# Projecting and normalising token slabs inside the attention loop of a two-layer mixer block

## Chip, cores and metric

One Trainium2 chip, all 8 cores. Each core computes one batch element with the same program; there is no traffic between cores. The metric is the device time of the slowest core in microseconds.

## What is computed

Two layers over x of 2048 tokens by 1024 features per batch element. Only the end of the first half of a layer matters here:

```python
for i in range(DEPTH):
    h = rms_norm(x, norm1_w[i])
    proj = h @ w_in[i]
    ...
    yd = diff_attn_mixer(pd, ...)        # causal, 4 heads, two score maps per head
    mix = jnp.concatenate([ya, yb, yc, yd], axis=-1)
    x = x + mix @ w_out[i]
    h = rms_norm(x, norm2_w[i])
    x = x + (silu(h @ ffn_w_gate[i]) * (h @ ffn_w_up[i])) @ ffn_w_down[i]
```

The differential attention takes, per head, two softmax maps p0 and p1 (32 features each for q and k), forms p0 - lam * p1, applies it to v (64 features), and normalises the result over each head's 64 features. Its 256 output features are the last quarter of `mix`.

## The kernel before

Everything is held transposed, features on partitions: xT (8 chunks of 128 features by 2048 tokens, fp32), hT (the normalised input, bf16) and mixT (bf16). Tokens are worked in four slabs of 512 (`NS = 4`). A layer goes through five mixer stages, then the projection by w_out with the second norm, then the FFN. Each engine runs its instructions in the order in which the program emits them; `Prog.op` works out the semaphore waits from the tiles read and written. For PSUM it takes whole 2 KB banks, whoever writes or reads them (`ap_region`).

PSUM has eight banks: psA has six, pst two. In the attention stage the scores rotate over `Sbanks` (L857: psA 0, psA 1, and half of pst), the accumulator of a head is psA 2 or 3 in turn (L887), psA 4 and 5 take the transposed outputs, and pst holds the sums and the transposes of the epilogue.

The attention stage is a list of units (L858 on): eight query blocks of 256 tokens (`qs`), in each four heads, in each the key blocks of 128 that the causal mask and the bias leave over. `emit_S` (L870) puts a unit's scores on TensorE: one matmul of 512 columns (two maps by 256 queries), and one more that adds the mask on the diagonal. `emit_exp_pv` (L883) has ScalarE take the exponential into SBUF, and TensorE multiply it with v into the head's bank; behind a head's last unit the bank is copied out, by ScalarE for even heads and VectorE for odd ones. The loop keeps two units ahead: unit u+2 has its scores emitted before unit u is retired (`retire`, L940). Later work of a head is put off by a count of retired units: three after its last unit its output is transposed (`emit_oT_transposes`, L893, 16 small transposes), and behind the fourth head's come `epilogue_a` (L901, a chain over VectorE and GpSimd) for the two 128-query blocks and, six units later, `epilogue_b` (L916: two transposes and a ScalarE copy into mixT).

The projection follows (L965 on): for each slab and each of 8 output chunks, 8 matmuls of 512 columns into one of six rotating banks (`psbank`, L419), and a VectorE add into xT. One slab behind it goes `norm_slab` (L452): 8 squares on ScalarE through two buffers, 8 matmuls with a matrix of ones, a logarithm, an exponential, and 8 VectorE multiplies into hT. The norm of the last slab is emitted behind that of the slab before it.

The FFN's weights come by GpSimd's queue in pieces (`load_group`, L988; slots of `load_piece`). The projection's two weight halves `pO` lie in slots 0 and 1, so the first gate piece (slot 0) waits for the last matmul on the first half, and the first up piece (slot 1) for the projection's last matmul. `ffn_gu` computes 8 gate matmuls and then 8 up matmuls per block of 128.

Of the kernel before, what the change touches and what calls it, by code (L numbers as in the profile page):

```python
# [11 lines left out]
AF = mybir.ActivationFunctionType  # L12
ALU = mybir.AluOpType
# [229 lines left out]
D = 1024  # L243
L = 2048
NT = 16
NS = 4
# [3 lines left out]
EPS = 1e-6  # L250
# [5 lines left out]
CP_N1W, CP_N2W, CP_CONVW, CP_CONVB, CP_DCOL, CP_SSMNW, CP_PSCALE, CP_QNW, CP_KNW, CP_BS = 0, 8, 16, 40, 46, 48, 50, 52, 53, 54  # L256
# [60 lines left out]
def build(nlayers=2, dbg=(), stop=None):  # L317
# [23 lines left out]
    def sb(name, shape, dt):  # L341
        return es.enter_context(nc.sbuf_tensor("s_" + name, list(shape), dt))
# [4 lines left out]
    P = Prog(nc, sem)  # L347

    xT = sb("xT", [128, 8, L], F32)
    hT = sb("hT", [128, 8, L], BF16)  # L350
    mixT = sb("mixT", [128, 8, L], BF16)
    arena = sb("arena", [128, ARENA], U8)
    cF = sb("cF", [128, NCF], F32)
    colp = sb("colp", [128, NCOLP], F32)
# [5 lines left out]
    onesb = sb("onesb", [128, 128], BF16)  # L360
    neghalf = sb("neghalf", [128, 1], F32)
    small = sb("small", [128, 64], F32)
    psA = es.enter_context(nc.psum_tensor("psA", [128, 6, 512], F32))
# [26 lines left out]
    def load_piece(slot, src, ncols, kind="in"):  # L390
        dst = ring_slot(slot, kind)
        if kind == "in":
            dst = dst[:, :, 0:ncols]
        else:
            dst = dst[:, 0:ncols, :]
        P.dma('pool', dst, src, 'ring%d' % slot, writes_sb=[dst])
        return dst
# [21 lines left out]
    def psbank(lo=0, hi=6):  # L419
        k = (lo, hi)  # L420
        v = psrot.get(k, 0)
        psrot[k] = v + 1
        return lo + v % (hi - lo)

    def load_x(fuse_norm):
        bm = Bump(arena, 16384, ARENA)
        stage = [bm.alloc([128, D], F32) for _ in range(4)]
        nbx = norm_bufs() if fuse_norm else None
        for t in range(NT):
            st = stage[t % 4]  # L430
            P.dma('sp', st, x_d[t * 128:(t + 1) * 128, :], 'xin%d' % (t % 4), writes_sb=[st])
            for half in range(2):
                b = psbank()
                for c4 in range(4):
                    c = half * 4 + c4
                    P.transpose(psA[:, b, c4 * 128:(c4 + 1) * 128], st[:, c * 128:(c + 1) * 128], identf)
                src = psA[:, b, :].rearrange("p (c t) -> p c t", c=4)
                dst = xT[:, half * 4:half * 4 + 4, t * 128:(t + 1) * 128]
                P.copy('act' if (t + half) % 2 == 0 else 'dve', dst, src)
            if fuse_norm and t % 4 == 3 and t >= 7:  # L440
                norm_slab(t // 4 - 1, CP_N1W, nbx)
        if fuse_norm:
            norm_slab(NS - 1, CP_N1W, nbx)

    def norm_bufs():
        bm = Bump(arena, 50 * 1024, ARENA)
        sq = [bm.alloc([128, 512], BF16) for _ in range(2)]
        ms = bm.alloc([128, 512], F32)
        rs = bm.alloc([128, 512], F32)
        return sq, ms, rs  # L450

    def norm_slab(s, nw_off, bufs):  # L452
        sq, ms, rs = bufs
        sl = slice(s * 512, (s + 1) * 512)
        b = psbank()
        for c in range(8):
            P.act(sq[c % 2], xT[:, c, sl], AF.Square)
            P.mm(psA[:, b, :], onesb[:], sq[c % 2], start=(c == 0), stop=(c == 7))
        P.act(ms, psA[:, b, :], AF.Ln, scale=1.0 / D, bias=EPS)
        P.act(rs, ms, AF.Exp, scale=-0.5)  # L460
        for c in range(8):
            P.stt(hT[:, c, sl], xT[:, c, sl], colp[:, nw_off + c:nw_off + c + 1], rs, ALU.mult, ALU.mult)

    def norm_full(nw_off):
        bufs = norm_bufs()
        for s in range(NS):
            norm_slab(s, nw_off, bufs)
# [23 lines left out]
    def layer(li, pre_normed=False):  # L491
# [95 lines left out]
        for cc in range(2):  # L587
            for s in range(NS):
                b = psbank()
                proj_fm(pC, cc * 128, s, b)  # L590
                P.copy('act', pcxs[cc][:, 16 + s * 512:16 + (s + 1) * 512], psA[:, b, :])
        for cc in range(2):
# [19 lines left out]
            for s in range(NS):  # L612
                sl = slice(s * 512, (s + 1) * 512)
                b = psbank()
# [46 lines left out]
        for zc in range(2):  # L661
            for s in range(NS):
                b = psbank()
# [166 lines left out]
        for blk in range(4):  # L830
            for s in range(NS):
                sl = slice(s * 512, (s + 1) * 512)
                b = psbank(0, 3)
# [12 lines left out]
        for t in range(NT):  # L846
            b = psbank()
            for dc in range(8):
# [3 lines left out]
        pO = [load_piece(0, w_out_d[li][:, 0:512].rearrange("(c p) n -> p c n", p=128), 512),  # L852
              load_piece(1, w_out_d[li][:, 512:1024].rearrange("(c p) n -> p c n", p=128), 512)]
# [29 lines left out]
        def emit_exp_pv(u, b):  # L883
            qs, h, kb, first, last = u
            e = 2 * qs - kb + 1
            P.act(PT[b], Sbanks[b], AF.Exp, bias=cF[:, CF_ALIBI + h * 17 + e:CF_ALIBI + h * 17 + e + 1])
            ob = 2 + (qs * 4 + h) % 2  # L887
            P.mm(psA[:, ob, :], vflat[:, kb, h * 65:h * 65 + 128], PT[b], start=first, stop=last)
            if last:
                ot = oTs[(qs * 4 + h) % 2]  # L890
                P.copy('dve' if h % 2 else 'act', ot[0:65, :], psA[0:65, ob, :])

        def emit_oT_transposes(qs, h):  # L893
            ot = oTs[(qs * 4 + h) % 2]
            for c in range(2):
                for j in range(2):
                    cols = slice(c * 256 + j * 128, c * 256 + (j + 1) * 128)
                    P.transpose(psA[:, 4 + j, (c * 4 + h) * 64:(c * 4 + h + 1) * 64], ot[0:64, cols], identf[0:64, 0:64])
                    P.transpose(psSum[:, j * 8 + c * 4 + h:j * 8 + c * 4 + h + 1], ot[64:65, cols], identf[64:65, 64:65])

        def epilogue_a(qb):  # L901
            j = qb % 2
            onb = onbs[j]
            P.recip(rc, psSum[:, j * 8:(j + 1) * 8])
            P.ts('dve', nr1, rc[:, 4:8], neglam, None, op0=ALU.mult)
            P.tt('dve', h4(o0), h4(psA[:, 4 + j, 0:256]), rc[:, 0:4].unsqueeze(2).to_broadcast([128, 4, 64]), ALU.mult)
            P.tt('dve', h4(o1), h4(psA[:, 4 + j, 256:512]), nr1.unsqueeze(2).to_broadcast([128, 4, 64]), ALU.mult)
            P.tt('pool', o0, o0, o1, ALU.add)
            P.tt('dve', o1, o0, o0, ALU.mult)
            P.rsum(ss4, h4(o1))  # L910
            P.ts('dve', ss4, ss4, 1.0 / 64, EPS, op0=ALU.mult, op1=ALU.add)
            P.tt('pool', rs4, ss4, neghalf[:, 0:1].to_broadcast([128, 4]), ALU.pow)
            P.tt('dve', h4(o1), h4(o0), rs4.unsqueeze(2).to_broadcast([128, 4, 64]), ALU.mult)
            P.stt(onb, o1, 1.0 - lam_init, rowp[:, RP_SUBLN:RP_SUBLN + 256], ALU.mult, ALU.mult)

        def epilogue_b(qb):  # L916
            ql = slice(qb * 128, (qb + 1) * 128)
            j = qb % 2
            ts0 = j * 2
            for jj in range(2):  # L920
                P.transpose(pst[:, ts0 + jj, :], onbs[j][:, jj * 128:(jj + 1) * 128], identb[:])
            P.copy('act', mixT[:, 6:8, ql], pst[:, ts0:ts0 + 2, :])

        pend = []
        deferred = []

        def fire(item):
            _, kind, args = item
            if kind == 'T':
                qs_, h_ = args  # L930
                emit_oT_transposes(qs_, h_)
                if h_ == 3:
                    epilogue_a(2 * qs_)
                    epilogue_a(2 * qs_ + 1)
                    deferred.append([6, 'E', 2 * qs_])
                    deferred.append([6, 'E', 2 * qs_ + 1])
            else:
                epilogue_b(args)

        def retire():  # L940
            pu, pb = pend.pop(0)
            emit_exp_pv(pu, pb)
            for d in deferred:
                d[0] -= 1
            ready = [d for d in deferred if d[0] <= 0]
            for d in ready:
                deferred.remove(d)
                fire(d)
            if pu[4]:
                deferred.append([3, 'T', (pu[0], pu[1])])  # L950

        for u in units:
            pend.append((u, emit_S(u)))
# [3 lines left out]
            retire()  # L957
        while deferred:
            fire(deferred.pop(0))

        if stop != 'D':
            dump('mix%d' % li, mixT)
# [1 line left out]

        nb = norm_bufs()  # L965
        for s in range(NS):
            sl = slice(s * 512, (s + 1) * 512)
            for c in range(8):
                half, cj = c // 4, c % 4
                b = psbank()  # L970
                for mc in range(8):
                    P.mm(psA[:, b, :], pO[half][:, mc, cj * 128:(cj + 1) * 128], mixT[:, mc, sl], start=(mc == 0), stop=(mc == 7))
                P.tt('dve', xT[:, c, sl], xT[:, c, sl], psA[:, b, :], ALU.add)
            if s >= 1:
                norm_slab(s - 1, CP_N2W, nb)
        norm_slab(NS - 1, CP_N2W, nb)

        dump('x1_%d' % li, xT)
        chk('wout')
# [174 lines left out]
```

How the kernel before makes its waits and increments, by code:

```python
        def run(engname, e):  # L157
            for waits, thunk, tok in plan[engname]:
                if thunk is None:
                    for s, v in waits:
                        e.wait_ge(semh[s], v)
                    continue
                for s, v in waits[:-1]:
                    e.wait_ge(semh[s], v)
                ins = thunk(e)
                if waits:
                    s, v = waits[-1]
                    ins._wait_ge(semh[s], v)
                if tok is None:
                    pass
                elif tok[0].startswith('d_'):
                    ins.then_inc(semh[tok[0]], 16)
                else:
                    ins.then_inc(semh[tok[0]], 1)
```

## Time and profile before

| | |
|---|---|
| time of three runs, median (lowest to highest) | 2531.61 us (2528.35 to 2532.37) |
| the profiled execution, time | 2531.23 us |
| its span on the slowest core | 2529.5 us |
| spans of the eight cores | 2520.7 to 2529.5 us |
| busy: TensorE / VectorE / ScalarE / GpSimd | 83% / 39% / 34% / 11% |
| mean granted clock of TensorE, slowest core | 0.893 |
| attention loop of the first layer | from about 427 to 719 us |
| projection and second norm of the first layer | from 724.4 to 800.7 us |

The slowest core's profile is read. Times in it count from the span's start. A clock of 1.00 is 2.4 GHz and 0.50 is 1.2 GHz. Durations come from the profiled execution. In the chain of waits a row is a start, a length and what the chain was in; a PE row's count is of matmuls in a row. "L197" is the helper through which all matmuls go, L212 that of ScalarE's activations, L215 and L225 those of VectorE and GpSimd element-wise operations, L201 that of transposes.

### The profile page before, as it was taken

The numbers are of one execution on the slowest core, as the hardware profiler recorded it, in microseconds if no ns is written. First come the engines' busy times: TensorE is split into PE (matmuls) and PEld (weight loads), VectorE is DVE, ScalarE is ACT, GpSimd is POOL, SyncE is SP. The second block draws the span as 40 slices with busy tenths as digits, with TensorE's granted clock in tenths as the row PEclk, the third lists the DMA queues.
The fourth block names the chain that finished last, engine by engine and source line by source line (L and its number), as shares of the span: only waits on it lengthen the run. The fifth ranks groups of instructions, "written<-read, shape, count | busy, mean of one in ns | idle before, by whom it ended". The sixth has DMA issues, their size and how long they took to land.

```text
span 2529.5 us, 26176 instructions; the slowest of 8 cores (2520.7 to 2529.5 us)
## 1 busy us (share of the span) xinstructions
PE 2091.8 (83%) x9828; PEld 926.2 (37%) x9828; DVE 986.1 (39%) x1912; ACT 870.4 (34%) x1512; POOL 281.2 (11%) x430
## 2 busy tenths in 40 slices
PE   5659558877879999999965875687787999999997
PEld 3224334322333444444322344243222344444443
DVE  3740563212125333333467136422111443333344
ACT  3524445456733111111143343545674211111111
POOL 0620320101000000000016023010000000000000
PEclk7869769788889999999988886878898999999999
DMA  6020102000006213210102010010000243221103
GB/s 172 1 35 1 26 1 34 0 1 1 0 1 92 46 19 50 46 22 9 28 1 34 1 26 1 10 24 1 0 1 0 29 71 51 36 43 23 26 1 133
DMA packets 56655, 69.19 MB, mean 27 GB/s; under 512 B 5456, under 2 KB 46416, under 8 KB 56528
## 3 DMA queue, kind: packets, MB, share of 16 engines
q0 software_dynamic: 51200, 49.63, 13.4%
q1 hardware_dynamic: 5328, 17.88, 2.0%
q8 instruction: 77, 1.26, 0.2%
q14 instruction: 50, 0.41, 0.1%
HBM read 108.75 MB, written 8.39 MB: 46 GB/s over the span
## 4 chain that ended last, share of the span: by engine, by line
PE 71%; DVE 13%; ACT 6%; POOL 5%; issue 3%; DMA 1%; SPq 0%; DVEq 0%; ACTq 0%; POOLq 0%
PE psA L197 65%; ACT s_arena L212 6%; DVE s_arena L215 5%; POOL s_arena L215 3%; DVE s_arena L225 3%; PE psA L201 3%; PE pst L201 2%; PE pst L197 2%; POOL s_small L215 1%; DVE s_hT L225 1%; DVE s_xT L215 1%; DMA s_arena<-x 1%; DVE s_small L237 1%; DVE s_small L221 1%; DMA out<-s_arena 0%
## 5 line engine op out<-in xcount | busy, mean ns | idle before, releaser
L197 PE MATMUL psA<-s_hT,s_arena 128*128 128x512 bf16 x3712 | 840.0, 385 | 2.3 <-ACT s_arena L212 2.3
L197 PE MATMUL psA<-s_arena 128*128 128x512 bf16 (+3 forms) x1662 | 401.9, 358 | 168.5 <-POOL s_arena L215 85.6
L197 PEld LDWEIGHTS psA<-s_hT,s_arena 128*128 128x128 bf16 x3712 | 367.8, 99 | 448.9 <-issue 23.4
L212 ACT ACTIVATE s_arena<-psA 128x512 bf16<-128x512 f32 (+1 forms) x354 | 210.0, 593 | 904.8 <-PE psA L197 904.7
L197 PE MATMUL psA<-s_mixT,s_arena 128*128 128x512 bf16 x1920 | 451.5, 386 | 13.4 <-DVE s_xT L215 12.8
L215 DVE TENSOR_TENSOR s_xT<-s_xT,psA 128x512 f32<-128x512 f32 x448 | 304.2, 687 | 120.6 <-PE psA L197 114.5
L215 DVE TENSOR_TENSOR s_mixT<-s_arena,psA 128x512 bf16<-128x512 bf16 x176 | 121.0, 688 | 479.4 <-PE psA L197 476.5
L197 PEld LDWEIGHTS psA<-s_arena 128*128 128x128 bf16 (+1 forms) x1662 | 128.1, 109 | 416.3 <-ACT s_arena L212 191.1
L197 PEld LDWEIGHTS psA<-s_mixT,s_arena 128*128 128x128 bf16 x1920 | 166.1, 99 | 288.6 <-DVE s_xT L215 125.2
L212 ACT ACTIVATE s_arena<-psA,s_cF 128x512 bf16<-128x512 f32 x352 | 228.8, 693 | 51.6 <-PE psA L197 51.2
L215 POOL TENSOR_TENSOR s_arena<-s_arena 128x256 f32<-128x256 f32 (+2 forms) x160 | 118.6, 742 | 733.1 <-DVE s_arena L215 666.8
L231 DVE COPY s_arena<-psA 65x512 f32<-65x512 f32 (+2 forms) x50 | 33.5, 670 | 376.3 <-PE psA L197 359.8
L197 PE MATMUL psA<-s_arena,s_onesb 128*128 128x512 bf16 x144 | 67.6, 492 | 84.5 <-ACT s_arena L212 79.9
L212 ACT ACTIVATE s_arena<-pst,s_cF 128x512 bf16<-128x512 f32 x174 | 120.5, 693 | 44.8 <-PE pst L197 44.6
L201 PE MATMUL psA<-s_cF,s_arena 64*128 64x64 f32 (+1 forms) x384 | 102.2, 323 | 27.5 <-DMA s_arena<-x 18.4
L212 ACT ACTIVATE s_arena<-s_arena 128x512 f32<-128x512 f32 (+2 forms) x150 | 92.0, 614 | 76.2 <-DVE s_arena L215 71.2
L212 ACT ACTIVATE s_arena<-s_xT 128x512 bf16<-128x512 f32 x128 | 73.3, 621 | 130.2 <-PE psA L197 119.3
L225 DVE SCALAR_TENSOR_TENSOR s_hT<-s_xT,s_colp,s_arena 128x512 bf16<-128x512 f32 x128 | 86.2, 747 | 72.6 <-ACT s_arena L212 72.6
L201 PE MATMUL pst<-s_identb,s_arena 128*128 128x128 bf16 x256 | 37.4, 259 | 90.0 <-DVE s_arena L225 69.2
L197 PE MATMUL psA<-s_arena,s_hT 128*128 128x512 bf16 (+2 forms) x768 | 97.5, 276 | 7.0 <-DVE s_arena L215 5.0
L201 PEld LDWEIGHTS psA<-s_cF,s_arena 64*128 64x128 f32 (+1 forms) x384 | 59.2, 163 | 56.9 <-issue 39.6
L142 POOL DMA_DIRECT2D s_arena<-ffn_w_gate x12 | 10.8, 898 | 595.7 <-PE psA L197 595.7
(82 smaller groups left out, 1310.0 us busy)
## 6 DMA issues: line engine op xcount, KB each, us to landing
s_arena<-ffn_w_gate POOLq DMA_DIRECT2D x10, 1024.0 KB, 10.3
s_arena<-ffn_w_up POOLq DMA_DIRECT2D x10, 1024.0 KB, 13.6
s_arena<-ffn_w_down POOLq DMA_DIRECT2D x10, 1024.0 KB, 8.3
s_arena<-x SPq DMA_DIRECT2D x16, 512.0 KB, 8.0
s_arena<-w_in POOLq DMA_DIRECT2D x8, 1024.0 KB, 9.9
out<-s_arena SPq DMA_DIRECT2D x16, 512.0 KB, 2.7
s_arena<-w_out POOLq DMA_DIRECT2D x4, 1024.0 KB, 8.6
s_arena<-w_in POOLq DMA_DIRECT2D x4, 512.0 KB, 11.9
```

The lines of the kernel that those rows point to most:

```text
L142: self.plan[queue].append((waits, (lambda e, o=out, i=in_, k=kw: e.dma_start(out=o, in_=i, **k)), tok))
L197: return self.op('pe', lambda e: e.matmul(out, lhsT, rhs, start=start, stop=stop, **kw), reads=[lhsT, rhs], writes=[out])
L201: return self.op('pe', lambda e: e.transpose(out, in_, ident), reads=[in_, ident], writes=[out])
L212: return self.op('act', lambda e: e.activation(out, in_, func, **kw), reads=rd, writes=[out])
L215: return self.op(eng, lambda e: e.tensor_tensor(out, in0, in1, op), reads=[in0, in1], writes=[out])
L221: return self.op(eng, lambda e: e.tensor_scalar(out, in0, s1, s2, op0, **kw), reads=[in0, s1, s2], writes=[out])
L225: return self.op('dve', lambda e: e.scalar_tensor_tensor(out, in0, scalar, in1, op0, op1), reads=[in0, scalar, in1], writes=[out])
L231: return self.op(eng, lambda e: e.tensor_copy(out, in_), reads=[in_], writes=[out])
L237: return self.op('dve', lambda e: e.reduce_sum(out, in_, AX.X), reads=[in_], writes=[out])
```

## The change

With `interleave` on (it is, in the full program), the projection of slabs 0 to 2 and their second norm are emitted inside the attention loop. Once `epilogue_b` has written the last block of a slab, nine items are queued: eight `wout_unit` (8 matmuls, one VectorE add) and one `norm_slab_inplace`. At each retired unit that isn't the last of its head, one item is taken and emitted behind the unit's value matmul. Its bank is the accumulator bank that the current head doesn't use. The norm takes its two square buffers from hT's last slab and writes logarithm and exponential in place in the PSUM bank, since the arena's norm buffers lie under the attention's tiles. Slab 3 is projected and normalised behind the loop as before.

```diff
-    def norm_slab(s, nw_off, bufs):
+    def norm_slab(s, nw_off, bufs, bank=None):
         sq, ms, rs = bufs
         sl = slice(s * 512, (s + 1) * 512)
-        b = psbank()
+        if bank is None:
+            bank = psA[:, psbank(), :]
...
+        interleave = stop is None
+        fill = []
+        wout_done = set()
+        fill_bank = [None]
+
+        def wout_unit(s_, c, bank=None):
+            sl = slice(s_ * 512, (s_ + 1) * 512)
+            half, cj = c // 4, c % 4
+            if bank is None:
+                bank = fill_bank[0]
+            for mc in range(8):
+                P.mm(bank, pO[half][:, mc, cj * 128:(cj + 1) * 128], mixT[:, mc, sl], start=(mc == 0), stop=(mc == 7))
+            P.tt('dve', xT[:, c, sl], xT[:, c, sl], bank, ALU.add)
+
+        def norm_slab_inplace(s_, nw_off, bank):
+            assert s_ < NS - 1
+            sl = slice(s_ * 512, (s_ + 1) * 512)
+            sq = [hT[:, 0, (NS - 1) * 512:NS * 512], hT[:, 1, (NS - 1) * 512:NS * 512]]
+            for c in range(8):
+                P.act(sq[c % 2], xT[:, c, sl], AF.Square)
+                P.mm(bank, onesb[:], sq[c % 2], start=(c == 0), stop=(c == 7))
+            P.act(bank, bank, AF.Ln, scale=1.0 / D, bias=EPS)
+            P.act(bank, bank, AF.Exp, scale=-0.5)
+            for c in range(8):
+                P.stt(hT[:, c, sl], xT[:, c, sl], colp[:, nw_off + c:nw_off + c + 1], bank, ALU.mult, ALU.mult)
+
+        def enqueue_slab(s_):
+            for c in range(8):
+                fill.append(lambda s_=s_, c=c: wout_unit(s_, c))
+            fill.append(lambda s_=s_: norm_slab_inplace(s_, CP_N2W, fill_bank[0]))
+            wout_done.add(s_)
...
                 epilogue_b(args)
+                if interleave and args % 4 == 3 and args // 4 < NS - 1:
+                    enqueue_slab(args // 4)
...
             if pu[4]:
                 deferred.append([3, 'T', (pu[0], pu[1])])
+            elif fill:
+                fill_bank[0] = psA[:, 2 + (pu[0] * 4 + pu[1] + 1) % 2, :]
+                fill.pop(0)()
...
+        while fill:
+            fill_bank[0] = psA[:, psbank(0, 4), :]
+            fill.pop(0)()
...
         for s in range(NS):
-            sl = slice(s * 512, (s + 1) * 512)
+            if s in wout_done:
+                continue
             for c in range(8):
-                half, cj = c // 4, c % 4
-                b = psbank()
-                for mc in range(8):
-                    P.mm(psA[:, b, :], pO[half][:, mc, cj * 128:(cj + 1) * 128], mixT[:, mc, sl], start=(mc == 0), stop=(mc == 7))
-                P.tt('dve', xT[:, c, sl], xT[:, c, sl], psA[:, b, :], ALU.add)
-            if s >= 1:
-                norm_slab(s - 1, CP_N2W, nb)
-        norm_slab(NS - 1, CP_N2W, nb)
+                wout_unit(s, c, bank=psA[:, psbank(), :])
+            norm_slab(s, CP_N2W, nb)
```

## Rows read from the trace of the kernel before

**Rows 1.** The page: busy time by engine, and the chain's shares.
```profile
PE 2091.8 (83%) x9828; PEld 926.2 (37%) x9828; DVE 986.1 (39%) x1912; ACT 870.4 (34%) x1512; POOL 281.2 (11%) x430
...
PE 71%; DVE 13%; ACT 6%; POOL 5%; issue 3%; DMA 1%; SPq 0%; DVEq 0%; ACTq 0%; POOLq 0%
```
**Rows 2.** Windows, first layer: busy time by engine, clock, DMA share, GB/s.
```profile
427.00:719.00 292.00, 230.28 (x872) 91.06 (x871) 54.88 (x153) 174.28 (x293) 26.59 (x31) 0.82 0.03 4
724.00:730.00 6.00, 5.96 (x17) 2.27 (x18) 0.69 (x1) 1.00 (x2) 0.00 (x0) 0.53 0.00 0
730.00:755.00 25.00, 25.00 (x117) 11.17 (x115) 9.88 (x15) 0.67 (x2) 0.00 (x0) 1.00 0.00 1
755.00:760.00 5.00, 3.70 (x14) 1.27 (x14) 0.43 (x1) 4.49 (x9) 0.00 (x0) 1.00 0.01 2
...
798.00:805.00 7.00, 6.70 (x15) 2.06 (x16) 5.62 (x10) 5.18 (x8) 0.00 (x0) 0.52 1.09 157
805.00:815.00 10.00, 10.00 (x48) 4.51 (x46) 5.07 (x8) 1.55 (x3) 0.00 (x0) 1.00 1.14 165
```
**Rows 3.** The chain of waits in a steady part of the loop.
```profile
646.13 0.22 PE pst L197
646.35 1.52 PE psA L197 x5
```
**Rows 4.** The chain of waits around an epilogue, at the end of query block 1.
```profile
482.36 0.44 DVE s_arena L225
...
482.94 0.39 PE pst L201 x2
...
486.52 2.13 PE psA L197 x5
```
**Rows 5.** Windows around the same epilogue, columns as in rows 2.
```profile
478.00:484.00 6.00, 0.98 (x6) 0.49 (x4) 2.59 (x8) 0.97 (x3) 1.74 (x2) 0.71 0.00 0
484.00:491.00 7.00, 7.00 (x21) 3.01 (x21) 0.69 (x1) 4.38 (x7) 0.00 (x0) 0.52 0.00 0
```
**Rows 6.** The chain of waits in the projection stage of the first layer.
```profile
724.41 30.31 PE psA L197 x128
...
754.74 0.70 DVE s_xT L215
755.44 0.05 issue
...
758.38 14.22 PE psA L197 x65
...
790.48 0.03 issue
...
800.69 14.47 PE psA L197 x57
```
**Rows 7.** Timeline of GpSimd: the issue of the first up piece.
```profile
790.77 0.87 POOL L142 DMA_DIRECT2D s_arena<-ffn_w_up  x1 [5.97 <-PE psA L197]
```
**Rows 8.** Landing of that piece, alone, and in the second layer (shortest of two).
```profile
DMA to landing us min/median/max: 12.0/12.0/12.0
...
DMA to landing us min/median/max: 12.2/15.0/17.8
```
**Rows 9.** The chain of waits in the projection stage of the second layer.
```profile
1948.46 29.28 PE psA L197 x128
...
2015.19 0.02 issue
...
2025.10 15.00 PE psA L197 x57
```
**Rows 10.** Timeline: one matmul of the loop, and the end of a norm.
```profile
645.97 0.38 PE L197 MATMUL pst<-s_arena 128*128 128x512 bf16 x1
...
758.81 0.60 ACT L212 ACTIVATE s_arena<-psA 128x512 f32<-128x512 f32 x1 [0.48 <-PE psA L197]
759.44 0.63 ACT L212 ACTIVATE s_arena<-s_arena 128x512 f32<-128x512 f32 x1
...
760.18 5.39 DVE L225 SCALAR_TENSOR_TENSOR s_hT<-s_xT,s_colp,s_arena 128x512 bf16<-128x512 f32 x8 [4.75 <-ACT s_arena L212]
```

More of the change, by code:

```diff
@@ L450, in norm_bufs @@
         return sq, ms, rs
-    def norm_slab(s, nw_off, bufs):
+    def norm_slab(s, nw_off, bufs, bank=None):
         sq, ms, rs = bufs
         sl = slice(s * 512, (s + 1) * 512)
-        b = psbank()
+        if bank is None:
+            bank = psA[:, psbank(), :]
         for c in range(8):
             P.act(sq[c % 2], xT[:, c, sl], AF.Square)
-            P.mm(psA[:, b, :], onesb[:], sq[c % 2], start=(c == 0), stop=(c == 7))
-        P.act(ms, psA[:, b, :], AF.Ln, scale=1.0 / D, bias=EPS)
+            P.mm(bank, onesb[:], sq[c % 2], start=(c == 0), stop=(c == 7))
+        P.act(ms, bank, AF.Ln, scale=1.0 / D, bias=EPS)
         P.act(rs, ms, AF.Exp, scale=-0.5)
@@ L925, in layer @@
         deferred = []
+        interleave = stop is None
[16 more added lines that the diff above has]
+                P.act(sq[c % 2], xT[:, c, sl], AF.Square)
+                P.mm(bank, onesb[:], sq[c % 2], start=(c == 0), stop=(c == 7))
+            P.act(bank, bank, AF.Ln, scale=1.0 / D, bias=EPS)
[7 more added lines that the diff above has]
+            wout_done.add(s_)
         def fire(item):
```

## The prediction

> **What bounds the kernel now.** I first read the page's totals and its chain of waits: TensorE (PE) is busy 83% of the span and carries 71% of the chain, so PE time, or time in which PE is made to wait, is what the end depends on [rows 1]. The windows then split the part of a layer that the change touches. The first layer's attention loop is 292 us long; in it PE is busy 230.3 us, ScalarE (ACT) 174.3 us, and the granted clock averages 0.82. The output projection after it runs at 117 matmuls in 25 us, 0.2137 us each, at the full 2.4 GHz [rows 2]. So the loop has 61.7 us without PE work, and the question is where they lie.
>
> The chain of waits and the timeline show two kinds of gap. In the steady loop the chain carries a score and a value matmul for each unit (one head, one block of 128 keys), six in 1.74 us, 0.58 us a unit, where two matmuls at 0.2137 take 0.43 [rows 3]. The rest, 0.15 us a unit, is PE waiting for the exponential. The long gaps are elsewhere: at the end of each pair of 128-query blocks, PE stands for about 5 us (0.98 us busy of 6) until VectorE (DVE) and GpSimd (POOL) have finished the second block's epilogue and its transposes start at 482.94 us [rows 4, 5]. After it the clock is at 1.2 GHz, and the chain has five matmuls in 2.13 us, 0.427 each [rows 4, 5].
>
> **What the change takes out.** Slabs 0 to 2 (512 tokens each) leave the stage behind attention. Before, the 128 matmuls of two slabs take 30.31 us from 724.41, and the projection's last matmul ends at 790.48; the norms of slabs 0 and 1 lie between [rows 6]. The last two norms then hold PE until 800.69, where the FFN starts, still at 1.2 GHz (0.52 in that window) [rows 2, 6]. Eight gate matmuls at 0.427 bring its first up matmul to about 804.1.
>
> After, slab 3 alone is left: 64 matmuls, the first 5.3 us of them at 1.2 GHz as in rows 2 (0.53 over 6 us), so about 16.3 us, ending at 724.4 + 16.3 = 740.7. One norm follows, about 4 us. But the FFN's second weight piece goes to the slot that the projection's last matmul reads. POOL issues it at 790.77, 0.29 us behind that matmul, and it lands 12.0 us later [rows 7, 8]. The first up matmul can start at 740.7 + 12.3 = 753.0 at the earliest, with PE idle from about 746.5. So **removing the norm of slab 2 from the end frees little: the transfer was hidden by two norms and now is not.** I add 2.1 us for a low clock after this idle time (before, the next window after 804 is at full speed). Saved: 804.1 − 753.0 − 2.1 = 49.0 us. In the second layer, by the same steps, the projection starts at 1948.46, ends at 2015.19, the piece lands 12.2 us after its issue, and the FFN starts at 2025.10 [rows 8, 9]; the low clock at the projection's start is shorter (29.28 us for its 128 matmuls), which makes about 50.5 us. **Together 99.5 us off.** SP's queue is not touched; POOL's epilogue work keeps its place, and its loads only move forward with the projection.
>
> **What it puts in.** The units retire in order, and every one that isn't the last of its head takes one fill. Counting them by the code (8, 16, 24, 31, 37, 43, 49 and 55 units for the eight query blocks of 256, numbered from 0): slab 0 is queued at unit 32, slab 1 at unit 87, slab 2 at unit 167, each right *behind* the long gap of its epilogue. Nine fills follow at once; none meets one of the 5 us gaps. So the matmuls fill only the 0.15 us a unit.
>
> (a) Eight groups of 8 matmuls per slab: 64 × 0.2137 = 13.7 us. All fills of a head use one bank, the other accumulator's. So the next group waits until DVE has added the last one: a matmul takes 0.38 us to its end, then 0.02, 0.70 for the add, 0.05 [rows 6, 10]. From one group's first matmul to the next: 7 × 0.2137 + 0.38 + 0.77 = 2.65 us; the ten matmuls of a fill and a unit are 2.14, which leaves 0.51; I take 0.56, as a weight load can stand in front. Six of the eight fills per slab wait so (one has the eight transpose pairs of the previous head before it, one is the first): 3.4 us. In slab 0 two of these waits are for the output copy of the head before, of the same size. Against it: eight bubbles of 0.15 filled, 1.2 us, and about 0.5 us once because ACT still has two scores ahead. Sum 13.7 + 3.4 − 1.7 = 15.4 us a slab, **46 us a layer**. Bounds: no waits at all, 36; waits and no bubbles, 52.
>
> Rows 2 show this stage with six rotating banks at 0.2137 us a matmul, no wait between groups. The Trainium skill (Perfetto Trace Analysis, Matmuls) says that independent groups should rotate through banks so that the evacuation overlaps the next group's matmuls. The change gives that up; were it kept, the sum would be 3 × 3.4 × 2 = 20 us lower, 2557. The bound "no waits at all" already covers this from the rows.
>
> (b) A norm in the loop. In the projection stage the ACT squares lie beside its matmuls except for about 4 us: from 754.74 to 758.38, where the ones-matmuls and the squares go to and fro over two buffers. The two activations after it (0.60, 0.63) and DVE's eight multiplies (5.39) lie beside the next slab's matmuls [rows 6, 10]. In the loop ACT runs in order: the next unit's exponential is queued behind all of it, PE's value matmul waits for that exponential, and the later scores wait behind it on PE. From the last fill: 1.2 to 1.9 us until the bank is free, 4.0, the last matmul's end 0.4, 1.3 for logarithm and exponential, 0.6 for the unit's own; about 8.1, of which three units (1.7 us) were there before: 6.4, and 5.8 where the bank is free sooner: **18.6 us a layer**. Bounds 15 and 20. No table is loaded: logarithm and exponential follow the squares and each other within 0.5 us, with no load between [rows 10]. Writing both back into PSUM in place is in no row; 0.60 us from PSUM to SBUF and 0.63 within SBUF are nearest, so I take them.
>
> (c) The bank stays held until DVE's eight multiplies end, 5.4 us. In slabs 0 and 2 the next head needs that bank after 6 and 5 units, 3.5 and 2.9 us: 2.0 + 2.6 = 4.6 us. In slab 1 it is ten units away: nothing. The head's DVE copy queues behind the multiplies, which lies in the same wait.
>
> (d) The clock. After ACT has held PE for 6 us with eight matmuls in them, it may fall, as it does after two norms (0.52 from 798 to 805) though not after one (1.00 from 755 to 760) [rows 2]. After an epilogue some 10 us go at 1.2 GHz (0.71 over 6 us, 0.52 over the next 7) [rows 5]; they hold 11.7 units of 0.854 us, which take 6.8 at full speed: 3.2 us. For (c) and (d) together between 3 and 14; I take **8 us a layer**, the drop in about half of the cases with the wait of (c) shorter then. That the fills begin at a low clock costs about 2 us a slab, and about as much returns, since dense matmuls end that stretch sooner: nothing, bounds −2 and +3 a slab.
>
> **Sum:** 2 × (46 + 18.6 + 8) = 145.2 in, 99.5 out, +46 us. The profiled execution took 2531.2 us (span 2529.5), 0.4 below the median of the three runs, 2531.6; so 2577.5.
>
> **Rivals.** *The gaps swallow the matmuls (faster).* If (a) cost nothing, because PE's 61.7 idle us a layer take up the 46, only (b), (c) and (d) remain: 2 × 26.6 − 99.5 = −46, 2485. The point from which it decides: the loop grows by less than 49.8 us a layer. For it: the idle time is large enough [rows 2]; against it: most of it lies at the epilogues, where no fill is taken. The Trainium skill (Perfetto Trace Analysis, Optimization Strategy) says that interleaving regimes whose busiest engine differs may improve performance; that rule would have this rival right. Chance 0.10.
> *The clock stays low around the fills.* Each norm fill drops it, and the groups after the epilogue run long at 1.2 GHz: 14 for (c) and (d), 3 × 3 more for the starts, 2 × (46 + 18.6 + 23) − 99.5 = +76, 2607. For it: every epilogue gap in the loop is followed by such a stretch. Chance 0.15.
> *The costs only just cancel:* 48 to 52 us more in each loop, by a shorter wait in (a) and no drop in (d). 2531, chance 0.04.
> *The norm at the end hides the transfer after all:* if the piece landed as late as before or earlier counted from the projection's end, my 49 would move by 5 us a layer at most; it is inside the range and gets no chance of its own.
> My forecast has 0.71.
>
> **Numbers.** Low end: (a) 43, (b) 15, (c, d) 3, twice, less 101, gives +21, 2552. High end: the clock rival, 2607. Faster by over 0.2% (5 us, about what a measurement tells from no change) has the first rival's 0.10; slower has the forecast and the clock rival, 0.86.
>
> **What would show it.** Right: attention stages of about 365 us instead of 292; PE waiting for DVE's adds into xT some 0.5 us about six times a slab; three gaps of PE of 4 to 6 us a layer behind squares; the FFN's first up matmul 12.3 us behind the projection's last one, with PE idle before it; the 5 us epilogue gaps as they were. Wrong: loops under 340 us, or fills that fall into epilogue gaps, or no wait for the second FFN piece.

## The result, and the profile after

The changed kernel takes **2584.68 us** (median of 9 runs) against 2532.55 us before (10 runs): a ratio of 1.022, interval 1.0195 to 1.0245. It is slower, by 52 us, where 46 were forecast. Some runs of most kernels, in which the granted clock of a die is lower, are longer by some per cent; they are in the medians, but not in the ratios, here and below. The profiled execution took 2586.25 us with a span of 2584.7 us.

The page of the changed kernel: span, busy time by engine, the chain by engine, then three groups of the costliest (busy time and mean ns, and behind the last bar the idle time before them).

```profile
span 2584.7 us, 26167 instructions; the slowest of 8 cores (2572.4 to 2584.7 us)
PE 2116.5 (82%) x9828; PEld 930.7 (36%) x9828; DVE 987.9 (38%) x1912; ACT 875.1 (34%) x1512; POOL 281.7 (11%) x430
PE 69%; DVE 14%; ACT 6%; POOL 5%; issue 3%; DMA 2%; SPq 0%; DVEq 0%; ACTq 0%; POOLq 0%
...
L197 PE MATMUL psA<-s_hT,s_arena 128*128 128x512 bf16 x3712 | 838.2, 384 | 14.1 <-DMA s_arena<-ffn_w_up 13.0
...
L197 PE MATMUL psA<-s_mixT,s_arena 128*128 128x512 bf16 x1920 | 468.9, 392 | 24.7 <-DVE s_xT L215 21.5
...
L212 ACT ACTIVATE s_arena<-psA,s_cF 128x512 bf16<-128x512 f32 x352 | 230.7, 692 | 108.4 <-PE psA L197 107.8
```

Against [rows 1], PE's count of instructions is the same and its share no higher. New are 13.0 us in which the FFN's matmuls wait for the up pieces. The wait of the projection's matmuls for VectorE's adds into xT is now 21.5 us; it was 12.8 before. ScalarE now waits 108 us for scores, 52 before.

**Where the time went.** The ScalarE copies that end each epilogue are marks that both traces have. Three of them are these, of the changed kernel (start, length, what, idle before it), with PE's transposes that the first waits for:

```profile
540.19 0.37 PE L201 MATMUL pst<-s_identb,s_arena 128*128 128x128 bf16 x2 [4.97 <-DVE s_arena L225]
...
540.66 0.37 ACT L230 COPY s_mixT<-pst 128x256 bf16<-128x256 bf16 x1 [5.03 <-PE pst L201]
...
750.99 0.37 ACT L230 COPY s_mixT<-pst 128x256 bf16<-128x256 bf16 x1 [4.85 <-PE pst L201]
...
799.26 0.37 ACT L230 COPY s_mixT<-pst 128x256 bf16<-128x256 bf16 x1 [4.74 <-PE pst L201]
```

The brackets show the 5 us gap of the epilogue, on PE 4.97 us, as long as ever: no fill fell into it. The times between the second copy of one query block of 256 and the next, in the first layer, for the kernels that follow as well (slab 0 is taken in the first stretch, slab 1 in the third, slab 2 in the fifth):

| from epilogue | before | changed | no_add | spaced | norm_out | gap_plain |
|---|---|---|---|---|---|---|
| 1 to 2 | 31.5 | 57.7 | 54.1 | 52.6 | 47.7 | 31.2 |
| 2 to 3 | 35.0 | 36.9 | 36.9 | 35.9 | 36.8 | 35.6 |
| 3 to 4 | 39.1 | 62.5 | 59.5 | 60.7 | 53.3 | 38.5 |
| 4 to 5 | 41.6 | 41.5 | 41.3 | 42.0 | 40.9 | 39.2 |
| 5 to 6 | 46.1 | 69.5 | 69.0 | 66.2 | 59.4 | 45.1 |
| 6 to 7 | 47.8 | 48.3 | 48.3 | 48.2 | 47.8 | 47.8 |
| sum over before | | +75.2 | +68.0 | +64.5 | +44.8 | −3.7 |
| the same, second layer | | +77.5 | +70.5 | +67.6 | +48.6 | −3.0 |

The first layer's loop grows by 75.2 us (77.5 in the second), 26.3, 23.4 and 23.4 us of it in the three stretches that take a slab, and the rest behind the first.

**Inside a stretch.** The chain of waits of the changed kernel, second slab: group, add, group.

```profile
585.20 0.70 DVE s_xT L215
585.90 0.05 issue
585.94 1.91 PE psA L197 x8
587.86 0.02 issue
587.88 0.70 DVE s_xT L215
588.58 0.05 issue
588.63 1.91 PE psA L197 x8
```

A period is 588.63 − 585.94 = 2.69 us. VectorE's add is on the chain in each, since the next group goes to the same bank. PE's visible idle time for it is 0.35 us a time, 16 times in the first layer's loop. In the projection stage before, with six banks, it was beside PE's work [rows 6].

The norm in the loop, third slab: the end of its chain, with ScalarE, then VectorE's eight multiplies, then PE.

```profile
708.69 0.62 ACT s_hT L212
709.31 0.04 issue
709.36 0.40 PE psA L197
709.76 0.02 issue
709.78 0.59 ACT psA L212
710.37 0.02 issue
710.40 0.59 ACT psA L212
...
711.09 5.37 DVE s_hT L225 x8
716.46 0.14 issue
716.59 1.24 PE psA L197 x5
```

The two activations in place in PSUM take 0.59 us each. The next head's first value matmul waits until the multiplies are through with its bank; PE is idle for 2.62 us there. Behind the squares PE has no single long gap: it stands for 0.44 us before the first ones-matmul, 0.51 and twice 0.20 us between them, and 1.45 us before its next value matmul.

**The end.** The chain from the projection of slab 3 to the FFN, first layer:

```profile
799.17 16.65 PE psA L197 x65
815.81 0.07 issue
815.89 12.41 DMA s_arena<-ffn_w_up
...
828.44 3.66 PE psA L197 x9
```

Before, the FFN's first matmuls, in the first and in the second layer, are these:

```profile
801.09 5.22 PE L197 MATMUL psA<-s_hT,s_arena 128*128 128x512 bf16 x15
...
2026.03 4.37 PE L197 MATMUL psA<-s_hT,s_arena 128*128 128x512 bf16 x10
```

Eight of them at 0.427 us are gate matmuls, so the first up matmul starts at 804.5 and 2029.4. From the projection's start to it is 29.3 us now, 80.1 before; in the second layer 2080.41 − 2051.66 = 28.8, before 81.0. That is 103.0 us saved in both. In: 75.2 + 77.5 = 152.7. The difference, about 50, is most of the 55 us between the two profiled executions. Of the rest, 2.5 us are the last transfer of the output, 5.19 us long instead of 2.70, and the low clock behind the two waits for the up pieces costs 3 to 4 us, an estimate from the clock over four microseconds behind each (0.67 from 829, 0.50 from 2080). Windows in the first layer:

```profile
817.00:829.00 12.00, 4.24 (x15) 1.52 (x16) 5.39 (x8) 5.32 (x8) 3.03 (x4) 0.82 0.97 131
829.00:833.00 4.00, 4.00 (x14) 1.49 (x12) 0.69 (x1) 0.00 (x0) 0.00 (x0) 0.67 1.06 168
```

(Changed kernel, columns as in rows 2: PE has 4.24 us of work in 12, and the granted clock is 0.67 in the four behind.)

### The profile page after: what moved, and what is told of

Same layout as the page of the kernel before. It is cut to its first block, busy times and chain, and to the rows that moved or that the text cites. A ratio compares the mean times of both kernels' runs of the same rounds, so it can differ in the third digit from the quotient of the medians.

```text
span 2584.7 us, 26167 instructions; the slowest of 8 cores (2572.4 to 2584.7 us)
## 1 busy us (share of the span) xinstructions
PE 2116.5 (82%) x9828; PEld 930.7 (36%) x9828; DVE 987.9 (38%) x1912; ACT 875.1 (34%) x1512; POOL 281.7 (11%) x430
## 4 chain that ended last, share of the span: by engine, by line
PE 69%; DVE 14%; ACT 6%; POOL 5%; issue 3%; DMA 2%; SPq 0%; DVEq 0%; ACTq 0%; POOLq 0%
PE psA L197 63%; DVE s_arena L215 5%; ACT s_arena L212 5%; POOL s_arena L215 3%; DVE s_arena L225 3%; PE psA L201 3%; PE pst L201 2%; DVE s_xT L215 2%; PE pst L197 2%; DVE s_hT L225 1%; POOL s_small L215 1%; DMA s_arena<-ffn_w_up 1%; DMA s_arena<-x 1%; DVE s_small L237 1%; DVE s_small L221 1%
## 5 line engine op out<-in xcount | busy, mean ns | idle before, releaser
L197 PE MATMUL psA<-s_arena 128*128 128x512 bf16 (+3 forms) x1662 | 411.2, 362 | 179.9 <-POOL s_arena L215 88.4
L197 PE MATMUL psA<-s_mixT,s_arena 128*128 128x512 bf16 x1920 | 468.9, 392 | 24.7 <-DVE s_xT L215 21.5
L201 PE MATMUL psA<-s_cF,s_arena 64*128 64x64 f32 (+1 forms) x384 | 103.8, 327 | 26.3 <-DMA s_arena<-x 17.8
L201 PE MATMUL pst<-s_identb,s_arena 128*128 128x128 bf16 x256 | 37.7, 261 | 89.0 <-DVE s_arena L225 69.5
L197 PE MATMUL psA<-s_arena,s_onesb 128*128 128x512 bf16 x96 | 47.3, 520 | 75.3 <-ACT s_arena L212 72.3
L197 PE MATMUL pst<-s_arena 128*128 128x512 bf16 x174 | 76.5, 440 | 0.0
L215 DVE TENSOR_TENSOR s_arena<-s_arena 128x256 f32<-128x256 f32 (+4 forms) x72 | 54.3, 754 | 52.7 <-POOL s_arena L215 29.0
L225 DVE SCALAR_TENSOR_TENSOR s_hT<-s_xT,s_colp,s_arena 128x512 bf16<-128x512 f32 x80 | 53.9, 746 | 52.6 <-ACT s_arena L212 52.6
```

The source lines that it names most:

```text
L197: return self.op('pe', lambda e: e.matmul(out, lhsT, rhs, start=start, stop=stop, **kw), reads=[lhsT, rhs], writes=[out])
L201: return self.op('pe', lambda e: e.transpose(out, in_, ident), reads=[in_, ident], writes=[out])
L215: return self.op(eng, lambda e: e.tensor_tensor(out, in0, in1, op), reads=[in0, in1], writes=[out])
L225: return self.op('dve', lambda e: e.scalar_tensor_tensor(out, in0, scalar, in1, op0, op1), reads=[in0, scalar, in1], writes=[out])
```

## The experiments

All are measured beside the kernel before. The ratios are of the same session's runs. The kernel before took 2531.9 to 2533.0 us in each session, so times of different sessions can be set beside each other.

**no_add: the adds left out.** Slabs 0 to 2 don't get the projected mix here.

```diff
-            P.tt('dve', xT[:, c, sl], xT[:, c, sl], bank, ALU.add)
+            if s_ == NS - 1:
+                P.tt('dve', xT[:, c, sl], xT[:, c, sl], bank, ALU.add)
```

> The VectorE adds of the projection into xT are left out for slabs 0 to 2 (so these tokens miss the projected mix); everything else is as changed. If the wait of the second group of a head for the one shared bank costs what I priced (six waits of about 0.56 us a slab, three slabs, two layers), this run is 20 us faster than the changed kernel, about 2565 us. Rival, that the matmuls as such don't fit between the exponentials and the wait for the bank only stands where PE would wait for ScalarE anyway: under 5 us faster. Rival, that the clock sets the extra time: the denser matmuls should bring it up, and more than 25 us go.

Measured: 2569.31 us, ratio 1.0135 (1.0083 to 1.0187), 15.4 us less than the changed kernel. The wait is real and on the path, smaller than priced. By the table the first layer's stretches of slabs 0 and 1 get 3.6 and 3.0 us shorter, near the price (3.4), that of slab 2 only 0.5; in the second layer slabs 0 and 1 give 3.2 and 4.5 us, and slab 2 takes 2.1 us more. The clock moved at the same time. These are the 12 us behind the norm of slab 2, in no_add (first row) and in the changed kernel (second):

```profile
699.00:711.00 12.00, 10.72 (x32) 4.49 (x33) 1.74 (x3) 6.34 (x10) 0.00 (x0) 0.57 0.00 0
```
```profile
716.50:728.50 12.00, 10.86 (x41) 4.17 (x42) 0.54 (x1) 8.87 (x15) 0.00 (x0) 0.86 0.00 0
```

During the norm itself the clock is 1.00 in both. Behind it no_add runs at 0.57 and gets 32 matmuls done in 12 us where the changed kernel, at 0.86, gets 41. In the stretch of slab 0 it is the other way round: mean clock 0.82 in no_add, 0.77 in the changed kernel. Only in that of slab 1 is it nearly the same, 0.87 and 0.88, and there the waits cost 3.0 us.

**norm_out: the norms out of the loop**, those of slabs 0 and 1 ahead of the projection of slab 3.

```diff
-            fill.append(lambda s_=s_: norm_slab_inplace(s_, CP_N2W, fill_bank[0]))
...
+        norm_slab(0, CP_N2W, nb)
+        norm_slab(1, CP_N2W, nb)
+        for c in range(8):
+            wout_unit(NS - 1, c, bank=psA[:, psbank(), :])
+        norm_slab(2, CP_N2W, nb)
+        norm_slab(3, CP_N2W, nb)
```

> Only the projections stay in the loop; the norms of slabs 0 and 1 are emitted behind the loop ahead of the projection of slab 3, the norm of slab 2 behind it, ahead of that of slab 3. My theory: out of the loop go 18.6 us (ScalarE held) and about 8 us (bank held, clock) a layer; behind it come two norms of about 5 us each that nothing hides, and the third stands in time that is spent waiting for the second FFN piece. So about 16 us a layer less than the changed kernel, 2552 us. Rival, that the norms cost nothing in the loop (ScalarE had spare time there): about 20 us more than the changed kernel, 2605 us.

Measured: 2546.78 us, ratio 1.0057 (1.0029 to 1.0086), 38 us less than the changed kernel, where 32 were expected. The loop now grows by 44.8 us in the first layer and 48.6 in the second, which is the price of the projection groups alone (46 forecast); the norms are the other 30.4 and 28.9 us (26.6 forecast). Behind the loop the two norms hold PE for about 12 us that nothing hides, 769.46 to 781.47; in the chain of norm_out, ScalarE and PE take turns:

```profile
770.50 0.62 PE psA L197
771.14 0.64 ACT s_arena L212
771.78 0.05 issue
```

and the projection of slab 3 begins at 781.47. It is still better than norms in the loop, where the attention's own exponentials stand behind them.

**spaced: a fill at every second unit.**

```diff
             elif fill:
-                fill_bank[0] = psA[:, 2 + (pu[0] * 4 + pu[1] + 1) % 2, :]
-                fill.pop(0)()
+                fill_gap[0] += 1
+                if fill_gap[0] % 2:
+                    fill_bank[0] = psA[:, 2 + (pu[0] * 4 + pu[1] + 1) % 2, :]
+                    fill.pop(0)()
```

> A fill at every second unit that may take one, instead of at every one. PE's added work is the same; the adds now lie under a whole unit, and ScalarE can run ahead. My theory: a fill adds about 1.4 us instead of 2.1, so 18 waits of 0.56 us and some bubbles a layer come back: 20 to 28 us less than the changed kernel, 2557 to 2565 us. Rival, that every fill costs its 8 matmuls whatever the distance: within 5 us of the changed kernel.

Measured: 2563.24 us, ratio 1.0114 (1.0044 to 1.0184), 21 us less than the changed kernel, the forecast's near end. The loop is 10.7 and 9.9 us shorter in the two layers, more than leaving out the adds gave (7.2 and 7.0). In its chain the groups and units run on, 11 and 13 matmuls without a wait, and the add shows only where a head ends:

```profile
581.31 2.39 PE psA L197 x11
583.72 0.70 DVE s_xT L215
...
584.56 2.96 PE psA L197 x13
```

**up_first: the order of the FFN's first pieces.** The up piece is issued first and goes into the third weight slot.

```diff
+            if gi == 0:
+                wu = load_piece(2, wu_d[li][:, 0:n * 128].rearrange("(c p) n -> p c n", p=128), n * 128)
+                wg = load_piece(0, wg_d[li][:, 0:n * 128].rearrange("(c p) n -> p c n", p=128), n * 128)
+                wd = load_piece(1, wd_d[li][0:n * 128, :].rearrange("(j p) n -> p j n", p=128), n, kind="down")
+                return wg, wu, wd
```

> The first up piece of the FFN goes into the third weight slot, free since the attention ended, and is issued first; the down piece takes the slot that the projection's last matmul frees. My theory: the wait of PE for that piece (12.4 us from the projection's last matmul, about 7 us of it idle) goes, and with it the low clock after it: 7 to 9 us a layer, 2567 to 2571 us. Rival, that the gate piece, issued later in this order and sharing the DMA engines, then lands as late: under 4 us in all.

Measured: 2565.75 us, ratio 1.0125 (1.0082 to 1.0168), 18.9 us less than the changed kernel, about 1 us more than the expected range. In the first layer the gate piece is now the transfer in the chain, but PE is idle for only 0.53 us before it, where it was idle for 7.1 us before the up piece; in the second layer PE waits for neither:

```profile
809.17 11.07 DMA s_arena<-ffn_w_gate
...
820.38 3.40 PE psA L197 x15
```

**before_up: the same order in the kernel before.** Edit as above.

> The kernel before the change, with the order of the FFN's first pieces of up_first: the up piece first, into the third slot. In up_first this took 18.9 us off the changed kernel. My theory: the wait for that piece exists only since the norm of slab 2 no longer stands between the projection's end and the FFN, so here it gains nothing, 2529 to 2535 us. Rival, that the order of the pieces is worth something in any case (a calmer DMA queue at the FFN's start): 2515 to 2525 us.

Measured: 2531.85 us against 2531.9, ratio 1.000 (0.9989 to 1.001). The order of the pieces is worth nothing where two norms stand between the projection and the FFN. The 18.9 us are a wait that the change made: 13.0 us of them are the idle time that the page shows, and part of the rest is the low clock behind it.

**gap_plain: groups at the epilogues instead of at the units.** The fill at each retired unit is dropped, three groups are taken at each epilogue of query blocks 2 to 6, the nine left over follow the loop, and the tail is that of norm_out. The edit, without `take_fills`, which takes a group for each bank it is given:

```diff
             for d in ready:
                 deferred.remove(d)
+                if d[1] == 'E':
+                    if d[2] % 2 == 0:
+                        take_fills([psA[:, 2 + (pu[0] * 4 + pu[1] + 1) % 2, :]])
+                    else:
+                        take_fills([psA[:, 4, :], psA[:, 5, :]])
                 fire(d)
```

> As norm_out, but the projection groups of slabs 0 to 2 are no longer taken one per unit. Three are taken at each epilogue of the query blocks 2 to 6: one ahead of the first epilogue transposes, in the spare accumulator bank, and two ahead of the second ones, in the two banks of the transposed outputs, which the epilogue has read by then. The nine that are left follow the loop. My theory: PE stands for 1.6 and 4.8 us there whatever happens, so these 15 groups a layer cost next to nothing, and the nine behind the loop 1.7 us each with several banks: 46 us a layer become about 16, so 60 us less than norm_out, 2487 us, less a few more where the denser matmuls keep the clock up. Rival, that the adds queued on VectorE behind the epilogue, and the next head's transposes behind them, give most of it back: 2525 to 2545 us.

Measured: 2479.06 us, ratio 0.9789 (0.9769 to 0.9809): 68 us less than norm_out, 53 less than the kernel before. In the loop 15 groups a layer cost less than nothing, −3.7 us (second layer −3.0). The timeline of PE at the epilogue of query block 2 shows the three groups, and only 0.76 us of the gap are left:

```profile
505.02 1.89 PE L197 MATMUL psA<-s_mixT,s_arena 128*128 128x512 bf16 x8
506.75 0.28 PE L201 MATMUL pst<-s_identb,s_arena 128*128 128x128 bf16 x2
506.86 3.62 PE L197 MATMUL psA<-s_mixT,s_arena 128*128 128x512 bf16 x16
511.23 0.28 PE L201 MATMUL pst<-s_identb,s_arena 128*128 128x128 bf16 x2 [0.76 <-DVE s_arena L225]
```

The groups also have other banks than in norm_out, so the wait for the one bank is gone with the placement; by no_add it is some 7 us of the 46, and the placement has the rest.

The clock is higher too. Windows behind the epilogue of query block 4 in the kernel before, and the same place in gap_plain:

```profile
589.00:596.00 7.00, 6.32 (x19) 2.87 (x19) 0.00 (x0) 4.40 (x8) 0.00 (x0) 0.50 0.00 0
```
```profile
586.00:596.00 10.00, 9.33 (x40) 3.71 (x40) 1.69 (x3) 8.83 (x16) 0.00 (x0) 1.00 0.01 2
```

That is the best of five places. Over the 10 us behind the second copy of query blocks 2 to 6, the clock was 0.67, 0.54, 0.62, 0.65 and 0.57 before and is 0.83, 0.66, 1.00, 0.83 and 0.66 now. Over the stretches of the table it is 0.90, against 0.84 before and 0.88 in norm_out. The 8 us beyond what I expected may come from this; no run separates them.

**gap_fill: the tail rebuilt too.** As gap_plain, but the nine groups left over go beside the last two epilogues, and the squares and ones-matmuls of the norms of slabs 0 to 2 are put between projection groups; up_first's order is used. The part of the edit behind the last epilogue:

```diff
+        gens = [norm_gen(1, S3, nb, 2), norm_gen(2, psA[:, 5, :], nb, 2)]
+        for c in range(8):
+            next(gens[c // 4])
+            wout_unit(NS - 1, c, bank=psA[:, psbank(0, 5), :])
+            if c % 4 == 3:
+                for _ in gens[c // 4]:
+                    pass
+        norm_slab(NS - 1, CP_N2W, nb)
```

(`norm_gen` emits two squares, yields, and then emits their two ones-matmuls, so that a projection group stands between.)

> As gap_plain, with the tail rebuilt too: the nine groups left go beside the last two epilogues, the squares and ones-matmuls of the norms of slabs 0 to 2 are put between projection groups so that ScalarE works beside them, and the first FFN up piece is issued first into the third weight slot. My theory: the loop as in gap_plain, the last nine groups fill the 12 us in which PE stood at the loop's end (3 us over), behind the last epilogue 17 us of projection and norms, 4 us of the last norm, then the FFN: 53 to 60 us a layer less than the kernel before, 2411 to 2425 us. Rival, that the gate piece or VectorE's adds and multiplies then set the tail's length: 2440 to 2460 us.

Measured: **2435.16 us, ratio 0.9618 (0.9604 to 0.9633)**, faster than both kernels, but 10 us short of what I expected. One cause is in its chain: behind the last matmul of the projection and of slab 2's norm, at 744.70, come the logarithm and exponential of slab 2 ahead of the last norm's squares on ScalarE, and the FFN starts at 752.12, 7.4 us later instead of 4:

```profile
744.70 0.61 ACT s_arena L212
...
745.33 1.16 ACT s_arena L212 x2
...
752.12 23.05 PE psA L197 x100
```

That is 3.4 us in the first layer. Another is at the loop's end: from the second copy of query block 6 to that of 7 it takes 53.0 us, 5.2 more than before, where 3 were expected. The rest stays open.

## Why the prediction was right, step by step

- **What bounds the loop, and where its gaps lie:** held. The gaps of 5 us stayed, and gap_plain shows that groups put there are free; at the units they are not (norm_out: +44.8 and +48.6 us for 24 groups a layer). The first layer's loop took about 367 us where 365 were forecast.
- **(a) 46 us a layer for the groups:** 44.8 and 48.6 measured. Its period (2.65 to 2.70) was 2.69. Its wait for the one bank was sized 10 us a layer, and 7.7 went when the adds were taken away, with the clock changed as well. The sentence from the Trainium skill (Perfetto Trace Analysis, Matmuls) on rotating banks agrees with the trace of the changed kernel, where the add is on the chain in every period. By no_add this wait is about a sixth of (a).
- **(b), (c), (d) 26.6 us a layer for norms in the loop:** 30.4 and 28.9 measured. The held ScalarE and the held bank show in the trace. In slab 2 PE is idle 2.62 us for the bank (2.6 priced); in slab 0, where 2.0 were priced, the first layer's trace has no such wait. The gap of 4 to 6 us behind the squares came in pieces of 0.2 to 1.5 us. The clock was the term left too small: it fell at the norm in all three slabs, not in half of them, at that of slab 0 for about 14 us:

```profile
514.00:528.00 14.00, 12.14 (x32) 4.15 (x31) 6.04 (x9) 9.15 (x16) 0.00 (x0) 0.51 0.00 0
...
610.00:617.00 7.00, 7.00 (x22) 3.22 (x22) 3.65 (x6) 3.61 (x6) 0.00 (x0) 0.53 0.00 0
...
719.00:723.00 4.00, 4.00 (x13) 1.56 (x12) 0.00 (x0) 2.59 (x4) 0.00 (x0) 0.58 0.00 0
```

  (Windows of the changed kernel; the clock is the first number behind POOL.) How the 30.4 us divide can be estimated from the windows over the table's stretches in the changed kernel and in norm_out:

```profile
482.93:799.26 316.33, 246.34 (x936) 94.40 (x937) 75.54 (x168) 168.64 (x284) 20.93 (x24) 0.84 0.00 1
```
```profile
483.67:769.54 285.87, 227.22 (x911) 88.52 (x911) 59.55 (x144) 150.41 (x254) 20.89 (x24) 0.88 0.00 1
```

  PE's idle time differs by 11 us and its busy time by 19. The 24 ones-matmuls are about 10 of the 19: in slab 2 four pairs of them take 0.59 and three times 0.91 us. The other 9 are left for the same matmuls taking longer, at a mean clock of 0.84 instead of 0.88. As an estimate that makes 21 us for (b) and (c), priced at 18.6 and up to 4.6, and 9 us for (d), to which the forecast left 3 to 4 of its 8. So the waits were sized a little too large and the clock too small. That the two partly cancel is luck.
- **99.5 us out:** 103.0 measured to the first up matmul, less the low clock behind it, 3 to 4 us. Small errors cancel here too. The FFN before starts at 801.09 and 2026.03, 0.4 and 0.9 us later than I read from the chain, whose last pieces begin with ones-matmuls; the projection of slab 3 took 16.6 us, where 16.3 were priced. The step that the gain rests on, that the second FFN piece lands 12 us behind the projection and is no longer hidden, is shown by the 12.41 us of DMA on the chain, by up_first (−18.9) and by before_up (0).
- **The rivals:** that the gaps swallow the matmuls fell for this placement, and is what gap_plain does with another. So the sentence on interleaving regimes (the Trainium skill, Perfetto Trace Analysis, Optimization Strategy) holds here only for work that is emitted where the busiest engine stands. The clock rival, 2607, was half right in that the clock fell at each norm, but the stretches were shorter than it needs.

## What to carry to other kernels

On an engine that runs in program order, moved work fills a bubble only if it is emitted at the bubble: 0.15 us at every unit is no room for a group of 1.7 us, while 1.6 and 4.8 us at an epilogue take three groups for nothing. Before moving a step away, ask what it was hiding: here a norm hid a weight transfer. And count what else the inserted work holds, its bank and, for a norm, the engine that the loop itself waits on.

## What the runs showed of the hardware beyond what I had expected

Filling PE's gap raised the clock behind it as well: over the 10 us behind the five filled epilogues from 0.54 to 0.67 up to 0.66 to 1.00, and over the loop from 0.84 to 0.90; 15 added groups a layer cost −3.7 and −3.0 us. And taking a wait away can move or lengthen such a fall: over the 12 us behind the norm of slab 2 the clock was 0.57 in no_add, where with the wait it had been 0.86, and most of that slab's gain went.
